# Two of four weight sums per head by accumulating DMAs, and the head loop in another order

## The chip, the cores and the metric

The kernel runs on one core of one Trainium2 chip, as a single program. The metric is the time of one execution on the device in microseconds; before the change the median of three runs is 1553.36 us (1551.82 to 1553.9). Engines are called PE (TensorE, matrix products), DVE (VectorE), ACT (ScalarE), POOL (GpSimd, which here only queues DMAs) and SP (SyncE, which queues nearly all DMAs). All hold their instructions in order and wait for each other with semaphores.

## The reference

A decoder trunk of two layers over 256 positions and a width of 2048, batch 1, in float32. Layer 0 is a multi-scale retention layer (8 heads), layer 1 a pooling mixer with four window widths; each is followed by a gated embedding, and a final RMSNorm ends it. The change touches layer 0 alone, and there the input projection and the work of a head:

```
q, k, v, g = split(rms_norm(x) @ w_in)          # per head 256 + 256 + 512 + 512 columns of w_in
q, k = rotate(q), rotate(k) / 16
y = (q k^T * decay) v                           # causal, decay per head
y = (y - mean(y)) / sqrt(var(y) + 1e-5)         # per head and position
h = x + (silu(g) * y) @ w_out                   # per head 512 rows of w_out
```

## The kernel before

All weights stream from memory once, as units of 128 partitions x 1024 values (512 KB; two blocks of 128 x 512). To keep float32 accuracy on PE, every unit is split: ACT casts it to float32r (`w_hi`, function `head_hi` in the head loop), DVE subtracts that from the original (`w_lo`, `head_lo`), and PE makes three products for each pair of blocks (hi x hi, hi x lo, lo x hi). `w_hi` and `w_lo` are rings of four units: the cast of unit u waits until PE has used unit u-4 (`unit_used`), the subtraction waits for the cast, PE waits for the subtraction (`lo_ready`).

Heads 1 to 7 are a loop of seven passes with 40 units each, in the order of the list `ORDER` (line 80). Four kinds of units are plain products: A (q and k columns; the first four, `h0` to `h3`, are half units), C (v columns), B (gate columns) and O (the output projection of the head before). A full unit has 12 matmuls of 128 x 512. The v and gate products over the first half of the inner dimension are made by a seven-product (Strassen-like) scheme, M1 to M7, each in two parts a and b with 6 matmuls. Their weights are blocks called X1 to X4, and for some products sums of such blocks: M1 uses X1, M3 X3, M2 X4; M5 uses X1+X2, M6 that plus X3, M4 that plus X4, and M7 X2+X3. There are thus four pairs (a, b) of sums per head, eight adds, all made by DVE into two buffers `t1_raw` and `t3_raw` (`t1_sum` to `t4_sum`, line 1235 and on; the arithmetic stands in `quad_sum`, line 1237).

Each pass loads 32 units (`HEAD_LOADS`, line 86: name, one of eight 512 KB slots, and the last unit that reads the slot). SP queues them in that order (`head_loads`, line 417); each load waits until the `w_lo` of the last reader of its slot's former content is done. Ahead of two named loads (`Y_TURN` and `QK_TURN`, line 93) SP queues the DMA transposes of the gated output y and of the rotated q and k ("turns"). ACT writes 16-bit halves for a turn (`y_halves`, `qk_halves`) and puts the transposed halves together afterwards (`y_words`, `qk_words`, which also cast to `oT_hi` and `qkT_hi`).

Where each piece of a head's own work stands among the units is written out by hand, as tests `if u == ...` in the functions `head` of ACT (line 1073) and DVE (line 1560); the order of PE's products stands in PE's `head` (line 635). What the prediction follows: `rotate` (rotary embedding of q, k out of PSUM), `fix_w`, `fix_c` and `fix_b` (what the seven products leave to add or subtract), `v_hi_part` and `v_lo_part` (v out of PSUM; the latter releases `c_read`, for which the output unit O2 waits, line 681), `scores` (line 576, waits for `qkT_ready`), `values`, `normalise` and `gate_y`.

Of the kernel before, what the change touches and what calls it, by code (L numbers as in the profile page):

```python
# [35 lines left out]
TT = 2  # L36
# [43 lines left out]
ORDER = ("h0 h1 h2 h3 A2 M1a A3 M1b A4 M3a A5 M3b A6 M5a A7 M5b "  # L80
         "C4 M6a C5 M6b C6 M7a C7 M7b O0 M4a O1 M4b B4 M2a M2b O2 O3 O4 O5 O6 O7 B5 B6 B7").split()
AT = {name: u for u, name in enumerate(ORDER)}
HEAD_S = len(ORDER)
IN_HEADS = (HEADS - 1) * HEAD_U // (2 * RAW)
MORE = (HEADS - 1) * (HEAD_S - HEAD_U)
HEAD_LOADS = (("A0", 3, "h1"), ("A1", 0, "h3"), ("A2", 1, "A2"), ("X1a", 2, "M1b"), ("X2a", 3, "M3b"), ("A3", 4, "A3"), ("X1b", 5, "M3a"),
# [4 lines left out]
SLOT = {name: slot for name, slot, _last in HEAD_LOADS}  # L91
LOADS_OF = {b: [name for name, slot, _last in HEAD_LOADS if slot == b] for b in range(2 * RAW)}
Y_TURN, QK_TURN = "C4", "O2"
SUM_OF = {"M5": 0, "M6": 4, "M7": 2, "M4": 6}
SUMS = 2 * FORMS
O_RET = -NC
# [35 lines left out]
def trunk(nc, stream, first0, first1, second, third, fourth, x, xT, pT, gains, pool_scale, final_gain, rope, decay, wider, counts, ident, out):  # L132
    with ExitStack() as ctx:
# [3 lines left out]
        def sem(name):  # L137
            return ctx.enter_context(nc.semaphore(name))
# [63 lines left out]
        v_lo = at("v_lo", 36, [P, TT, COL], F32R)  # L202
        t1_raw = at("t1_raw", 32, [P, UNIT, UNIT * COL], F32)
        t3_raw = at("t3_raw", 24, [P, UNIT, UNIT * COL], F32)
        snap_s1 = at("snap_s1", 46, [P, COL], F32)
# [89 lines left out]
        c_read = sem("c_read")  # L295
        t_ready = sem("t_ready")
        snap_ready = sem("snap_ready")
        c_fixed = sem("c_fixed")
# [44 lines left out]
        def load_of(name):  # L343

            if name[0] == "h":
                return f"A{int(name[1]) // 2}"
            if name[0] == "M":
                return {"M1": "X1", "M3": "X3", "M2": "X4"}[name[:2]] + name[2]
            return name

        def unit_raw(name):

            if name[0] == "h":
                return slot(SLOT[load_of(name)])[:, int(name[1]) % 2 * COL:(int(name[1]) % 2 + 1) * COL]
            if name[:2] == "M7":
                return t3_raw[:, "ab".index(name[2]), :]
            if name[:2] in ("M5", "M6", "M4"):
                return t1_raw[:, "ab".index(name[2]), :]
            return slot(SLOT[load_of(name)])
# [105 lines left out]
        @block.gpsimd  # L465
        def _(pool):
            pool.wait_ge(xT_landed[NC - 1], 16)
            pool.dma_start(idn[:], ident).then_inc(idn_landed, 16)
            pool.dma_start(gain[:], gains).then_inc(gain_landed, 16)
            pool.dma_start(pscale[:], pool_scale).then_inc(pscale_landed, 16)  # L470

            pool.wait_ge(rope_landed, 32)
            pool.dma_start(dec[:], decay).then_inc(dec_landed, 16)
            pool.dma_start(p_raw, pT).then_inc(p_landed, 16)

            pool.wait_ge(yT_done, 1)
            pool.dma_start(wide[:], wider).then_inc(inv_landed, 16)
            pool.dma_start(inv[:], counts).then_inc(inv_landed, 16)

            pool.wait_ge(d_ready, 2 * GROUPS)  # L480
            pool.dma_start(fgain[:], final_gain).then_inc(fgain_landed, 16)
# [3 lines left out]
        def _(pe):  # L485
# [149 lines left out]
            def head(hd, base):  # L635
# [40 lines left out]
                g_unit(4, base)  # L676
                product_part("M2a", base, acc["B"][0][:], *a12, False)
                product_part("M2b", base, acc["B"][0][:], *a12, False)
                pe.wait_ge(snap_ready, hd * 3)
# [11 lines left out]
                pe.wait_ge(b_fixed, hd * 2)  # L691
                g_unit(5, base)
                g_unit(6, base)
# [135 lines left out]
        def _(act):  # L829
# [11 lines left out]
            def head_hi(hd, u, base):  # L841

                name = ORDER[u]
                act.wait_ge(unit_used, base + (u + 1 - RING))
                if name[:2] not in SUM_OF and name not in ("h1", "h3"):
                    wait_head_landed(act, hd, load_of(name))
                if name[:2] in SUM_OF:
                    act.wait_ge(t_ready, hd * SUMS + (SUM_OF[name[:2]] + "ab".index(name[2]) + 1 - SUMS))
                dst = w_hi[:, u % RING, 0:COL] if u < HALVES else w_hi[:, u % RING, :]
                act.copy(dst, unit_raw(name)).then_inc(hi_ready, 1)  # L850
# [98 lines left out]
            def qk_words(hd, base):  # L949
                act.wait_ge(yT_ready, hd)  # L950
                words_of(hd * 2 - 1, in_emb, words)
                act.wait_ge(words_ready, hd * 4)
                act.wait_ge(lo_ready, base + (AT["M7b"] + 1))
                for b in range(2):
                    act.copy(qkT_hi[:, 2 * b:2 * b + 2, :], words[:, 2 * b:2 * b + 2, :]).then_inc(qkT_hi_ready, 1)
# [117 lines left out]
            def head(hd, base):  # L1073
                for u in range(HEAD_S):
                    head_hi(hd, u, base)
                    if u == 3:
                        g_sigmoid(hd - 1, base)
                    if u == 6:
                        y_halves(hd - 1)
                    if ORDER[u] == "A6":  # L1080
                        snapshot(snap_s1, base + (AT["M1b"] + 1))
                    if u == 14:
                        y_words(hd - 1)
                    if u == 21:
                        qk_halves(hd)
                    if ORDER[u] == "C7":
                        snapshot(snap_u2, base + (AT["M6b"] + 1))
                    if u == 25:
                        qk_words(hd, base)
                    if u == 26:  # L1090
                        snapshot(snap_u3, base + (AT["M7b"] + 1))
                    if u == 30:
                        act.wait_ge(lo_ready, base + (AT["M4b"] + 1))
                        act.wait_ge(c_fixed, hd * 2)
                        v_hi_part(hd, base + (AT["C7"] + 1))
# [129 lines left out]
        def _(dve):  # L1225
# [12 lines left out]

            def t1_sum(hd, i):
                ab = "ab"[i]  # L1240
                wait_head_landed(dve, hd, "X1" + ab)
                wait_head_landed(dve, hd, "X2" + ab)
                quad_sum(hd, t1_raw[:, i, :], slot(SLOT["X1" + ab]), slot(SLOT["X2" + ab]))

            def t3_sum(hd, i):
                ab = "ab"[i]
                wait_head_landed(dve, hd, "X3" + ab)
                quad_sum(hd, t3_raw[:, i, :], slot(SLOT["X2" + ab]), slot(SLOT["X3" + ab]))

            def t2_sum(hd, i, base):  # L1250
                dve.wait_ge(lo_ready, base + (AT[("M5a", "M5b")[i]] + 1))
                quad_sum(hd, t1_raw[:, i, :], t1_raw[:, i, :], slot(SLOT[("X3a", "X3b")[i]]))

            def t4_sum(hd, i, base):
                dve.wait_ge(lo_ready, base + (AT[("M6a", "M6b")[i]] + 1))
                wait_head_landed(dve, hd, ("X4a", "X4b")[i])
                quad_sum(hd, t1_raw[:, i, :], t1_raw[:, i, :], slot(SLOT[("X4a", "X4b")[i]]))

# [121 lines left out]
            def rotate(hd, done, a_reads, tiles=range(TT)):  # L1380
# [15 lines left out]
                if TT - 1 not in tiles:  # L1396
                    return
                ins.then_inc(a_read, 1)
                dve.wait_ge(a_read, a_reads)
                dve.tensor_tensor(qk[:], qk[:], qk2[:], ALU.add).then_inc(qk_ready, 1)  # L1400
# [159 lines left out]
            def head(hd, base):  # L1560
                for u in range(HEAD_S):
                    head_lo(u, base)
                    if u == 4:
                        gate_y(hd - 1)
                    if u in (6, 8):
                        t1_sum(hd, (u - 6) // 2)
                    if u in (10, 12):
                        t3_sum(hd, (u - 10) // 2)
                    if u in (14, 16):
                        t2_sum(hd, (u - 14) // 2, base)  # L1570
                    if u in (22, 24):
                        t4_sum(hd, (u - 22) // 2, base)
                    if u == 21:
                        y_lo_part(hd - 1, False)
                    if u in (18, 19):
                        rotate(hd, base + (AT["A7"] + 1), hd * 3 - 1, (u - 18,))
                    if u == 26:
                        qkT_lo_part(hd, False)
                    if u == 28:
                        fix_w(hd, base)  # L1580
                    if u == 29:
                        fix_c()
                    if u == 31:
                        v_lo_part(hd)
# [319 lines left out]
```

## Time and profile before

| what | us |
|---|---|
| median of three runs | 1553.36 |
| the profiled execution | 1553.85 |
| its span, from first to last instruction | 1551.6 |
| PE busy | 1531.0 |
| DVE busy | 1153.2 |
| ACT busy | 926.6 |
| POOL busy | 4.6 |
| one pass of the head loop (259.00 to 348.43) | 89.43 |

The profile is of one execution, and its times are its own; it took 0.49 us more than the median of the runs. PE's busy time counts pipelined matmuls, whose ends are modelled, so small delays are best read from the starts of successive matmuls in the timeline. The seven passes of the head loop lie between 78.80 and some 705 us. PE's granted clock is 1.00 in every stretch of the head loop.

### The profile page before, as it was taken

What the parts mean: (1) busy time and instruction counts of PE and PEld (TensorE: products, weight loads), DVE (VectorE), ACT (ScalarE), POOL (GpSimd) and SP (SyncE); (2) the same over time, 40 slices, a digit from 0 to 9 for tenths busy, and PEclk for the clock granted to TensorE, in tenths of its full rate; (3) what the DMA queues carried; (4) which work ended last, traced back from release to release, by engine and by line L of the source; (5) the groups of instructions that cost most, each with busy time, mean ns of one, the idle gap of its engine ahead of it and who ended that gap; (6) DMA issues with size and microseconds to landing.
All of it is one profiled execution on the core that took longest, in us unless ns stands there. A gap on an engine that the chain in (4) does not pass through costs nothing.

```text
span 1551.6 us, 19968 instructions
## 1 busy us (share of the span) xinstructions
PE 1531.0 (99%) x6788; PEld 1259.3 (81%) x6788; DVE 1153.2 (74%) x1418; ACT 926.6 (60%) x1108; POOL 4.6 (0%) x12
## 2 busy tenths in 40 slices
PE   9999999999999999999999999999999999999997
PEld 7777878888887888888888888888888888888885
DVE  6989888888979888997766675775577557755665
ACT  7466574747566474756767556644664476446843
POOL 0000000000000000000000000000000000000000
PEclk9999999999999999999999999999999999999998
DMA  9485665757666565765566657655765576555651
GB/s 383 162 255 181 208 200 186 203 174 232 202 215 187 181 201 193 217 212 200 194 206 228 199 208 210 224 197 196 222 213 200 189 216 219 216 204 186 219 195 74
DMA packets 133498, 318.42 MB, mean 205 GB/s; under 512 B 80545, under 2 KB 80561, under 8 KB 112337
## 3 DMA queue, kind: packets, MB, share of 16 engines
q1 hardware_dynamic: 132608, 314.35, 60.9%
q0 software_dynamic: 704, 3.27, 0.5%
q8 instruction: 25, 0.41, 0.1%
q10 hardware_dynamic: 144, 0.26, 0.0%
q14 instruction: 17, 0.13, 0.0%
HBM read 297.40 MB, written 2.10 MB: 193 GB/s over the span
## 4 chain that ended last, share of the span: by engine, by line
PE 75%; DVE 10%; issue 6%; ACT 4%; DMA 4%; SPq 1%; ACTq 0%; DVEq 0%
PE accA L493 9%; PE accA L494 9%; PE accA L495 9%; PE accC L493 9%; PE accC L494 8%; PE accC L495 8%; PE accB L493 5%; PE accB L494 5%; PE accB L495 5%; DVE w_lo L1232 3%; DMA halvesT_e<-halves_e 2%; DMA w_raw<-in_stream_dram 2%; ACT w_hi L850 1%; ACT words_e L929 1%; DVE t_raw L1237 1%
## 5 line engine op out<-in xcount | busy, mean ns | idle before, releaser
L1311 DVE TENSOR_TENSOR w_lo<-w_raw,w_hi 128x1024 fp32r<-128x1024 f32 x326 | 395.8, 1222 | 227.8 <-ACT w_hi L839 226.0
L839 ACT CAST w_hi<-w_raw 128x1024 fp32r<-128x1024 f32 x326 | 340.0, 1052 | 267.9 <-PE accA L495 100.7
L850 ACT CAST w_hi<-w_raw 128x1024 fp32r<-128x1024 f32 (+1 forms) x224 | 219.5, 998 | 166.2 <-PE accC L495 50.5
L1232 DVE TENSOR_TENSOR w_lo<-w_raw,w_hi 128x1024 fp32r<-128x1024 f32 (+1 forms) x224 | 255.4, 1152 | 61.1 <-ACT w_hi L850 60.4
L493 PE MATMUL accA<-w_hi,xa_hi 128*128 128x512 f32 x452 | 176.2, 390 | 1.0 <-DVE w_lo L1311 0.6
L495 PE MATMUL accA<-w_hi,xa_lo 128*128 128x512 f32 x452 | 175.9, 389 | 0.0
L494 PE MATMUL accA<-w_lo,xa_hi 128*128 128x512 f32 x452 | 175.9, 389 | 0.0
L493 PE MATMUL accC<-w_hi,xa_hi 128*128 128x512 f32 x396 | 155.0, 391 | 0.5 <-DVE w_lo L1232 0.2
L494 PE MATMUL accC<-w_lo,xa_hi 128*128 128x512 f32 x396 | 154.2, 389 | 0.0
L495 PE MATMUL accC<-w_hi,xa_lo 128*128 128x512 f32 x396 | 154.1, 389 | 0.0
L493 PEld LDWEIGHTS accA<-w_hi,xa_hi 128*128 128x128 f32 x452 | 84.8, 188 | 19.7 <-DVE w_lo L1232 1.1
L495 PEld LDWEIGHTS accA<-w_hi,xa_lo 128*128 128x128 f32 x452 | 84.8, 188 | 17.6
L494 PEld LDWEIGHTS accA<-w_lo,xa_hi 128*128 128x128 f32 x452 | 84.8, 188 | 17.5
L493 PEld LDWEIGHTS accC<-w_hi,xa_hi 128*128 128x128 f32 x396 | 74.3, 188 | 18.9 <-DVE w_lo L1232 3.4
L495 PEld LDWEIGHTS accC<-w_hi,xa_lo 128*128 128x128 f32 x396 | 74.3, 188 | 15.6
L494 PEld LDWEIGHTS accC<-w_lo,xa_hi 128*128 128x128 f32 x396 | 74.3, 188 | 15.2
L1232 DVE TENSOR_TENSOR w_lo<-t_raw,w_hi 128x1024 fp32r<-128x1024 f32 x56 | 68.3, 1219 | 14.0 <-ACT w_hi L850 14.0
L493 PE MATMUL accC<-w_hi,oT_hi 128*128 128x512 f32 x184 | 72.4, 394 | 5.5 <-DVE v_lo L1423 5.5
L493 PE MATMUL accA<-w_hi,oT_hi 128*128 128x512 f32 x184 | 72.4, 394 | 0.2
L494 PE MATMUL accC<-w_lo,oT_hi 128*128 128x512 f32 x184 | 71.7, 390 | 0.0
L495 PE MATMUL accC<-w_hi,oT_lo 128*128 128x512 f32 x184 | 71.7, 390 | 0.0
L495 PE MATMUL accA<-w_hi,oT_lo 128*128 128x512 f32 x184 | 71.6, 389 | 0.0
(277 smaller groups left out, 2947.4 us busy)
## 6 DMA issues: line engine op xcount, KB each, us to landing
w_raw<-in_stream_dram SPq DMA_DIRECT2D x162, 1024.0 KB, 4.8
w_raw<-in_stream_dram SPq DMA_DIRECT2D x224, 512.0 KB, 4.9
h<-in_x_dram SPq DMA_DIRECT2D x4, 512.0 KB, 13.3
xT_raw<-in_xT_dram SPq DMA_DIRECT2D x3, 512.0 KB, 14.4
dec<-in_decay_dram POOLq DMA_DIRECT2D x1, 1024.0 KB, 9.2
fgain<-in_final_gain_dram POOLq DMA_DIRECT2D x1, 1024.0 KB, 7.1
out_dram<-emb SPq DMA_DIRECT2D x1, 1024.0 KB, 3.8
halvesT_e<-halves_e SPq DMA_TRANSPOSE x56, 6.1
```

The costliest lines, as they stand in the source:

```text
L493: pe.matmul(acc[pair][t][:, 0:n], xh, wh, start=first and b == 0, stop=False, skip_group_check=onto)
L494: pe.matmul(acc[pair][t][:, 0:n], xh, wl, start=False, stop=False, skip_group_check=onto)
L495: mm = pe.matmul(acc[pair][t][:, 0:n], xl, wh, start=False, stop=last and b == UNIT - 1, skip_group_check=onto)
L839: act.copy(w_hi[:, r % RING, :], w_raw[:, r // 2, (r % 2) * 1024:(r % 2 + 1) * 1024]).then_inc(hi_ready, 1)
L850: act.copy(dst, unit_raw(name)).then_inc(hi_ready, 1)
L929: act.copy(dst[:].bitcast(U16).rearrange("p k (n two) -> p two k n", two=2)[:, i, :, :], bufs[1][:, 4 * i:4 * i + 4, :]).then_inc(words_re ...
L1232: dve.tensor_tensor(w_lo[:, u % RING, 0:n], unit_raw(ORDER[u]), w_hi[:, u % RING, 0:n].bitcast(F32), ALU.subtract).then_inc(lo_ready, 1)
L1237: dve.tensor_tensor(dst, in0, in1, ALU.add).then_inc(t_ready, 1)
L1311: dve.tensor_tensor(w_lo[:, r % RING, :], w_raw[:, r // 2, (r % 2) * 1024:(r % 2 + 1) * 1024], w_hi[:, r % RING, :].bitcast(F32), ALU.subt ...
```

## The change

Two of the four pairs of sums are no longer made by DVE. POOL queues four DMAs a head that add a block from memory onto a block that lies in its slot: X2 onto X1 (a and b, once M1 has used X1) for M5, and X3 onto X2 (once X2 has landed) for M7. DVE makes the other two pairs in place: X3 onto the X1 slots for M6, and X4 for M4. `t1_raw` and `t3_raw` go, and so two waits of ACT that guarded their memory. The stream's blocks are ordered anew with `HEAD_LOADS`, the slots are given out anew, both turns stand at other loads, PE makes B5 ahead of M2b, and many pieces of ACT's and DVE's head work stand at other units.

```
-         "C4 M6a C5 M6b C6 M7a C7 M7b O0 M4a O1 M4b B4 M2a M2b O2 O3 O4 O5 O6 O7 B5 B6 B7").split()
+         "C4 M6a C5 M6b C6 M7a C7 M7b O0 M4a O1 M4b B4 M2a B5 M2b O2 O3 O4 O5 O6 O7 B6 B7").split()
-HEAD_LOADS = (("A0", 3, "h1"), ("A1", 0, "h3"), ("A2", 1, "A2"), ("X1a", 2, "M1b"), ("X2a", 3, "M3b"), ("A3", 4, "A3"), ("X1b", 5, "M3a"),
...
+HEAD_LOADS = (("A0", 3, "h1"), ("A1", 2, "h3"), ("A2", 1, "A2"), ("X1a", 0, "M4a"), ("A3", 3, "A3"), ("X1b", 6, "M4b"), ("A4", 5, "A4"),
+              ("X3a", 4, "M5b"), ("A5", 7, "A5"), ("X3b", 2, "M6a"), ("A6", 1, "A6"), ("X2a", 3, "M7a"), ("A7", 5, "A7"), ("X2b", 7, "M7b"),
+              ("C4", 1, "C4"), ("C5", 5, "C5"), ("C6", 4, "C6"), ("C7", 1, "C7"), ("X4a", 2, "M2a"), ("X4b", 5, "M2b"), ("O0", 4, "O0"),
+              ("O1", 3, "O1"), ("B4", 1, "B4"), ("B5", 4, "B5"), ("O2", 0, "O2"), ("O3", 1, "O3"), ("O4", 2, "O4"), ("O5", 3, "O5"), ("O6",
+              4, "O6"), ("O7", 5, "O7"), ("B6", 6, "B6"), ("B7", 7, "B7"))
-Y_TURN, QK_TURN = "C4", "O2"
-SUM_OF = {"M5": 0, "M6": 4, "M7": 2, "M4": 6}
+Y_TURN, QK_TURN = "C5", "B4"
+DMA_SUM = {"M5": "X1", "M7": "X2"}
+SUM_OF = {"M6": 0, "M4": 2}
@@ POOL
+            def add_block(hd, base, x, term, used):
+                n = names.index(term + x[2])
+                at = hd * (HEAD_U // (2 * RAW)) + ((RET1 - HEAD_U + n) // (2 * RAW))
+                pool.wait_ge(lo_ready, base + (AT[used] + 1))
+                pool.dma_start(slot(SLOT[x]), rounds[at, n // 2 % RAW, :, n % 2 * UNIT * COL:(n % 2 + 1) * UNIT * COL],
+                               accum_op=ALU.add).then_inc(sum_landed[x], 16)
+            def head_sums(hd, base):
+                add_block(hd, base, "X1a", "X2", "M1a")
+                add_block(hd, base, "X1b", "X2", "M1b")
+                wait_head_landed(pool, hd, "X2a")
+                add_block(hd, base, "X2a", "X3", "M1b")
+                wait_head_landed(pool, hd, "X2b")
+                add_block(hd, base, "X2b", "X3", "M1b")
@@ PE, head
                 product_part("M2a", base, acc["B"][0][:], *a12, False)
+                g_unit(5, base)
                 product_part("M2b", base, acc["B"][0][:], *a12, False)
...
-                g_unit(5, base)
@@ ACT, head_hi
+                if name[:2] in DMA_SUM:
+                    act.wait_ge(sum_landed[DMA_SUM[name[:2]] + name[2]], hd * 16)
@@ ACT, head: the unit behind which each piece stands
-  g_sigmoid 3, y_halves 6, y_words 14, qk_halves 21, qk_words 25, v_hi_part 30
+  g_sigmoid 4, y_halves 8, y_words 19, qk_halves 23, qk_words 28, v_hi_part 29
@@ DVE, head: the same
-  gate_y 4, t1_sum 6 and 8, t3_sum 10 and 12, rotate 18 and 19, y_lo_part 21, qkT_lo_part 26, fix_w 28, fix_c 29, v_lo_part 31
+  gate_y 6, rotate 17 and 19, its sum (rotated) 20, y_lo_part 23, qkT_lo_part 31, fix_w 27, fix_c 28, v_lo_part 30
```

The last four lines put the diff's tests `if u == ...` in a row. `t2_sum` (behind units 14 and 16) and `t4_sum` (22 and 24) stay at their places and now add in place into the X1 slots.

## Rows read from the trace of the kernel before

**Rows 1.** The page: one engine's busy time (1), the main DMA queue (3).
```profile
PE 1531.0 (99%) x6788; PEld 1259.3 (81%) x6788; DVE 1153.2 (74%) x1418; ACT 926.6 (60%) x1108; POOL 4.6 (0%) x12
...
q1 hardware_dynamic: 132608, 314.35, 60.9%
```
**Rows 2.** Stretches: length, busy, clock, DMA share, GB/s; five heads' sum.
```profile
900.00:1000.00 100.00, 100.00 (x443) 82.81 (x442) 63.71 (x66) 60.82 (x67) 0.00 (x0) 1.00 0.66 213
...
259.00:348.43 89.43, 88.55 (x394) 72.71 (x393) 77.52 (x98) 54.07 (x60) 0.00 (x0) 1.00 0.63 199
...
sum 446.93, PE 442.74 PEld 363.59 DVE 387.78 ACT 270.40 POOL 0.00; mean PE 88.55 PEld 72.72 DVE 77.56 ACT 54.08 POOL 0.00
```
**Rows 3.** PE's waits: line, waited for, us in total, times, longest.
```profile
PE accC L493 <- DVE v_lo L1423: 5.5, 7, 0.8
```
**Rows 4.** Timeline of PE, head 259.00: start, duration, line, operation (before C6, O1, O2).
```profile
287.56 0.39 PE L525 MATMUL side<-w_hi,f_hi 128*128 128x512 f32 x1
...
288.92 0.39 PE L493 MATMUL accC<-w_hi,xa_hi 128*128 128x512 f32 x1
...
296.85 0.39 PE L527 MATMUL side<-w_hi,f_lo 128*128 128x512 f32 x1
297.28 0.50 PE L493 MATMUL accC<-w_hi,xa_hi 128*128 128x512 f32 x1
...
309.43 0.39 PE L527 MATMUL accB<-w_hi,xa_lo 128*128 128x512 f32 x1
309.85 0.50 PE L493 MATMUL accA<-w_hi,oT_hi 128*128 128x512 f32 x1
...
320.73 0.28 PE L586 MATMUL side<-qkT_hi,qkT_lo 128*128 128x128 f32 x1
321.81 0.49 PE L493 MATMUL accC<-w_hi,oT_hi 128*128 128x512 f32 x1 [0.80 <-DVE v_lo L1423]
```
**Rows 5.** Timeline of DVE, same head: an add, and O1's subtraction.
```profile
268.05 1.22 DVE L1237 TENSOR_TENSOR t_raw<-w_raw 128x1024 f32<-128x1024 f32 x1
...
308.57 1.23 DVE L1232 TENSOR_TENSOR w_lo<-w_raw,w_hi 128x1024 fp32r<-128x1024 f32 x1 [2.20 <-ACT w_hi L850]
```
**Rows 6.** Timeline of ACT, same head.
```profile
287.83 1.06 ACT L850 CAST w_hi<-w_raw 128x1024 fp32r<-128x1024 f32 x1 [0.68 <-PE accA L495]
...
296.12 2.00 ACT L919 COPY halves_e<-qk 128x1024 uint16<-128x1024 uint16 x2 [1.80 <-DVE qk L1400]
...
303.74 2.60 ACT L929 COPY words_e<-halvesT_e 128x1024 uint16<-128x1024 uint16 x2 [0.82 <-DMA halvesT_e<-halves_e]
...
307.50 1.04 ACT L850 CAST w_hi<-w_raw 128x1024 fp32r<-128x1024 f32 x1
...
316.89 1.27 ACT L910 ACTIVATE v_hi<-accC,rs 128x512 fp32r<-128x512 f32 x2 [2.93 <-DVE accC L1299]
318.05 3.88 ACT L850 CAST w_hi<-w_raw 128x1024 fp32r<-128x1024 f32 x4
```
**Rows 7.** Line 432, the head's plain loads (35 issued between 268 and 362 us).
```profile
DMA to landing us min/median/max: 3.5/4.8/7.6
```
**Rows 8.** The page (6): loads from POOL's queue, KB each, us to landing.
```profile
fgain<-in_final_gain_dram POOLq DMA_DIRECT2D x1, 1024.0 KB, 7.1
...
sig<-in_pT_dram POOLq DMA_DIRECT2D x1, 512.0 KB, 12.3
```
**Rows 9.** Timeline of SP, same head: the two turns, each with the load behind it.
```profile
272.23 1.26 SPq L414 DMA_TRANSPOSE halvesT_e<-halves_e  x1
...
278.18 1.54 SPq L432 DMA_DIRECT2D w_raw<-in_stream_dram  x3
...
298.21 1.24 SPq L414 DMA_TRANSPOSE halvesT_e<-halves_e  x1
...
301.93 0.38 SPq L432 DMA_DIRECT2D w_raw<-in_stream_dram  x1
```
**Rows 10.** Groups of DVE, same head: busy, mean ns, idle before and its releaser.
```profile
L1232 DVE TENSOR_TENSOR w_lo<-w_raw,w_hi 128x1024 fp32r<-128x1024 f32 (+1 forms) x32 | 36.4, 1151 | 9.0 <-ACT w_hi L850 8.9
```

More of the change, by code:

```diff
@@ L85 @@
 MORE = (HEADS - 1) * (HEAD_S - HEAD_U)
-HEAD_LOADS = (("A0", 3, "h1"), ("A1", 0, "h3"), ("A2", 1, "A2"), ("X1a", 2, "M1b"), ("X2a", 3, "M3b"), ("A3", 4, "A3"), ("X1b", 5, "M3a"),
[4 rows of a table removed]
+HEAD_LOADS = (("A0", 3, "h1"), ("A1", 2, "h3"), ("A2", 1, "A2"), ("X1a", 0, "M4a"), ("A3", 3, "A3"), ("X1b", 6, "M4b"), ("A4", 5, "A4"),
[4 rows of a table added]
 SLOT = {name: slot for name, slot, _last in HEAD_LOADS}
 LOADS_OF = {b: [name for name, slot, _last in HEAD_LOADS if slot == b] for b in range(2 * RAW)}
-Y_TURN, QK_TURN = "C4", "O2"
-SUM_OF = {"M5": 0, "M6": 4, "M7": 2, "M4": 6}
-SUMS = 2 * FORMS
+Y_TURN, QK_TURN = "C5", "B4"
+DMA_SUM = {"M5": "X1", "M7": "X2"}
+SUM_OF = {"M6": 0, "M4": 2}
+SUMS = 4
 O_RET = -NC
@@ L202, in trunk @@
         v_lo = at("v_lo", 36, [P, TT, COL], F32R)
-        t1_raw = at("t1_raw", 32, [P, UNIT, UNIT * COL], F32)
-        t3_raw = at("t3_raw", 24, [P, UNIT, UNIT * COL], F32)
         snap_s1 = at("snap_s1", 46, [P, COL], F32)
@@ L296, in trunk @@
         t_ready = sem("t_ready")
+        sum_landed = {x: sem(f"sum_landed_{x}") for x in ("X1a", "X1b", "X2a", "X2b")}
         snap_ready = sem("snap_ready")
@@ L347, in load_of @@
             if name[0] == "M":
-                return {"M1": "X1", "M3": "X3", "M2": "X4"}[name[:2]] + name[2]
+                return {"M1": "X1", "M5": "X1", "M6": "X1", "M4": "X1", "M7": "X2", "M3": "X3", "M2": "X4"}[name[:2]] + name[2]
             return name
@@ L354, in unit_raw @@
                 return slot(SLOT[load_of(name)])[:, int(name[1]) % 2 * COL:(int(name[1]) % 2 + 1) * COL]
[L355 to L358, printed above, removed]
             return slot(SLOT[load_of(name)])
@@ L466, in _ @@
         def _(pool):
+            rounds = stream.rearrange("(i s) p n -> i s p n", s=RAW)
+            names = [name for name, _slot, _last in HEAD_LOADS]
+            def add_block(hd, base, x, term, used):
[11 more added lines that the diff above has]
+                add_block(hd, base, "X2b", "X3", "M1b")
             pool.wait_ge(xT_landed[NC - 1], 16)
@@ L474, in _ @@
             pool.dma_start(p_raw, pT).then_inc(p_landed, 16)
+            for hd in range(1, HEADS):
+                head_sums(hd, hd * HEAD_S + (RET1 - HEAD_S))
             pool.wait_ge(yT_done, 1)
@@ L844, in head_hi @@
                 act.wait_ge(unit_used, base + (u + 1 - RING))
-                if name[:2] not in SUM_OF and name not in ("h1", "h3"):
+                if name[:2] not in SUM_OF and name[:2] not in DMA_SUM and name not in ("h1", "h3"):
                     wait_head_landed(act, hd, load_of(name))
+                if name[:2] in DMA_SUM:
+                    act.wait_ge(sum_landed[DMA_SUM[name[:2]] + name[2]], hd * 16)
                 if name[:2] in SUM_OF:
@@ L952, in qk_words @@
                 act.wait_ge(words_ready, hd * 4)
-                act.wait_ge(lo_ready, base + (AT["M7b"] + 1))
                 for b in range(2):
@@ L1075, in head @@
                     head_hi(hd, u, base)
-                    if u == 3:
+                    if u == 4:
                         g_sigmoid(hd - 1, base)
-                    if u == 6:
+                    if u == 8:
                         y_halves(hd - 1)
@@ L1081, in head @@
                         snapshot(snap_s1, base + (AT["M1b"] + 1))
-                    if u == 14:
+                    if u == 19:
                         y_words(hd - 1)
-                    if u == 21:
+                    if u == 23:
                         qk_halves(hd)
@@ L1087, in head @@
                         snapshot(snap_u2, base + (AT["M6b"] + 1))
-                    if u == 25:
+                    if u == 28:
                         qk_words(hd, base)
@@ L1091, in head @@
                         snapshot(snap_u3, base + (AT["M7b"] + 1))
-                    if u == 30:
-                        act.wait_ge(lo_ready, base + (AT["M4b"] + 1))
+                    if u == 29:
                         act.wait_ge(c_fixed, hd * 2)
@@ L1237, in quad_sum @@
                 dve.tensor_tensor(dst, in0, in1, ALU.add).then_inc(t_ready, 1)
[L1239 to L1248, printed above, removed]
             def t2_sum(hd, i, base):
                 dve.wait_ge(lo_ready, base + (AT[("M5a", "M5b")[i]] + 1))
-                quad_sum(hd, t1_raw[:, i, :], t1_raw[:, i, :], slot(SLOT[("X3a", "X3b")[i]]))
+                x1 = slot(SLOT[("X1a", "X1b")[i]])
+                quad_sum(hd, x1, x1, slot(SLOT[("X3a", "X3b")[i]]))
             def t4_sum(hd, i, base):
@@ L1256, in t4_sum @@
                 wait_head_landed(dve, hd, ("X4a", "X4b")[i])
-                quad_sum(hd, t1_raw[:, i, :], t1_raw[:, i, :], slot(SLOT[("X4a", "X4b")[i]]))
+                x1 = slot(SLOT[("X1a", "X1b")[i]])
+                quad_sum(hd, x1, x1, slot(SLOT[("X4a", "X4b")[i]]))
             def form_sums(i):
@@ L1398, in rotate, with rotated @@
                 ins.then_inc(a_read, 1)
+                if len(tiles) == TT:
+                    rotated(a_reads)
+            def rotated(a_reads):
                 dve.wait_ge(a_read, a_reads)
@@ L1562, in head @@
                     head_lo(u, base)
-                    if u == 4:
+                    if u == 6:
                         gate_y(hd - 1)
[L1565 to L1568, printed above, removed]
                     if u in (14, 16):
@@ L1572, in head @@
                         t4_sum(hd, (u - 22) // 2, base)
-                    if u == 21:
+                    if u in (17, 19):
+                        rotate(hd, base + (AT["A7"] + 1), hd * 3 - 1, ((u - 17) // 2,))
+                    if u == 20:
+                        rotated(hd * 3 - 1)
+                    if u == 23:
                         y_lo_part(hd - 1, False)
-                    if u in (18, 19):
-                        rotate(hd, base + (AT["A7"] + 1), hd * 3 - 1, (u - 18,))
-                    if u == 26:
+                    if u == 31:
                         qkT_lo_part(hd, False)
+                    if u == 27:
+                        fix_w(hd, base)
                     if u == 28:
-                        fix_w(hd, base)
-                    if u == 29:
                         fix_c()
-                    if u == 31:
+                    if u == 30:
                         v_lo_part(hd)
```

4 rows, old and new, of the table HEAD_LOADS are left out of this document.

## The prediction

> **What bounds the kernel now.** I read the page's first part first: TensorE (PE) is busy for 99% of the span [rows 1]. The table by stretches shows where the rest is: a stretch of the pool stage has no idle PE, while five heads of the head loop take 446.93 us, 89.39 each, with PE idle about 1% [rows 2]. PE's list of waits has one long row, 5.5 us in seven pieces, for `v_lo` of VectorE (DVE) [rows 3]. The timeline of PE in the head from 259.00 to 348.43 shows the losses. Where nothing is late a matmul starts every 0.227 us (six in 1.36) [rows 4]. At C6 the first matmul starts 0.43 after the one ahead of it, 0.20 late, and takes 0.50 in place of 0.39: 0.31 us. At O1 it is 0.19 and 0.11: 0.30. At O2, behind the scores' short matmuls (0.11 apart), 0.97 and 0.10: 1.07. That is 1.68 us in a head that is as long as the mean, 11.8 us in seven heads, and all that this change can win: 0.76% of the run. DVE as a whole is not short of time (77.5 of 89.4 us), but each gap ends on it, or on ScalarE (ACT), which feeds it.
>
> **What it removes.** Per head eight adds on DVE (`t_raw`) become four; each takes DVE 1.22 us [rows 5], so it has 4.9 us less to do. That pays only where a gap waits for DVE; PE's own work is unchanged.
>
> *O2's gap.* `fix_c` stood behind unit 29, `v_hi` behind cast 30, `v_lo` behind unit 31, the one just ahead of O2, and PE waited for its end. Each now stands a unit earlier, and B5, M2b and the scores lie between: `v_lo` follows the `w_lo` of B5, when PE has B5 (2.72), M2b (1.36) and the scores (1.3) still to do. It is two operations of half a unit's size; up to 5 us would be hidden. `qkT_lo`, now behind unit 31, is as large and has M2b's 1.36 of cover: just in time for the scores. I take the whole 1.07 as won.
>
> *O1's gap.* ACT made the qk words (303.74 to 307.50) ahead of O1's cast; the cast started at 307.50, its `w_lo` at 308.57, PE at 309.85 [rows 4 to 6]. The words now come behind cast 28. Heads differ here; I take 0.25 as won.
>
> **What it adds: 28 accumulating DMAs of 512 KB from POOL's queue.** The trace has none. From below: a plain load of that size lands 3.5 us after issue at the least. From above: POOL's `sig` load, stuck behind others, took 12.3 [rows 7, 8]. I take 7.1, that of POOL's 1 MB load, since an add has to read the old block and the addend. The first pair has least time. X1a's add starts when the `w_lo` of M1a is done, some 6 us after the head's start, and lands at 13. Unit starts follow from 1.36 and 2.72 a unit, and a cast starts 0.27 after the successor of the unit that frees its ring slot (287.83 against 287.56 [rows 4, 6]): cast M5a may start at 18.0, M5b at 22.0, where X1b's add, from 11, lands at 18. PE is held only by a cast that starts later than 2.35 before its unit (1.07 to `w_lo`, 1.28 to PE), so 12.3 costs nothing either; some 15 us are the limit. The adds of X2a and X2b have more. Behind their waits only each other is queued.
>
> The Trainium skill (Collectives: The Full Stack, "The bandwidth ceiling: the fold count and why AG ≠ RS ≠ AR") says that a DMA that adds reads two sources through one ring and so moves at half a copy's rate. By it the sum stays as it is, and the engines pay twice a load for each add; no run here shows it yet.
>
> **The y turn and C6.** Here I expect the change to pay something back. Times from the head's start: cast A6 waits for A4's matmuls (16.33), starts at 16.6, its `w_lo` ends at 18.9, and only then does SP issue C4's load, at 19.0, and the y turn, at 19.6. (Before, the turn began at 13.2, 272.23.) Its two transposes hold SP for 5.95 us (272.23 to 278.18), those of the qk turn 3.72 (298.21 to 301.93) [rows 9]. So C5 is issued between 23.3 and 25.6 and, with the median of 4.8 [rows 7], lands between 28.1 and 30.4. Behind it ACT casts C5 and M6b (0.95 each), makes y's words as it makes qk's (3.76), then casts C6: PE can start C6 0.1 + 1.9 + 3.76 + 2.35 = 8.1 after C5's landing. Without a gap its turn is at 38.1, so C5 must land by 30.0. The quick turn gives no gap, the slow one 0.4 and the restart's 0.1. I take 0.56 (C5 at 30.5), 0.25 more than now: nearer to the slow turn, since two loads and an add are in flight ahead of it.
>
> **B5.** From the end of O0: 0.27, cast B4 0.95, qk's words 3.76, cast M2a 0.95, `v_hi` 1.16, then 2.35, in sum 9.4. PE has M4a, O1, M4b, B4 and M2a, 9.5, until it wants B5. There is no slack, and B4's load now stands behind the qk turn. From C5's landing at 30.5 ACT has six casts, y's words, a snapshot of half a cast's size and the qk halves (2.0 [rows 6]): to 42.4. The turn's 3.72 and a landing of 4.8 give 50.9; the cast could have started at 49.6 + 0.56 + 0.27 = 50.4. I take 0.35 lost; the range is 0 to 0.9.
>
> The other moves (gate, y halves, rotation in two parts, later O units) lie beside units for which DVE has time to spare (ahead of its `w_lo` it waits 9.0 us a head, 8.9 of them for ACT's casts [rows 10]); I cost them at nothing. If that lead is gone, PE waits for `w_lo` between A4 and M5b.
>
> **Sum.** Per head -1.07 - 0.25 + 0.25 + 0.35 = -0.72; in seven -5.0 us. The profiled execution took 1553.85 us (span 1551.6 and 2.25 around it): 1548.8. It lies 0.49 above the median of the runs: 1548.3.
>
> **Rivals.** (1) *C5 lands late, because the adds share the DMA engines with the turn: slower.* X2b lands at 20 to 22; its add then runs until 27 to 30, over the transposes and C5's load. The loads' queue took 60.9% of the span for 314.35 MB [rows 1], 1.6 us for 512 KB; an add of twice that takes 3.2. If C5 bears half of it, the gap grows by 1.6, if all, by 3.2: -0.72 + 1.6 = +0.88 a head, 1559.5, or +2.48, 1570.7; between them 1565. It decides from C5 at 31.2 on. For: landings reach 7.6 [rows 7], and a turn can last 2.2 us longer than another. Against: the engines are idle for over a third of the span, and X2b's add is not wanted before 39.
>
> The Trainium skill (DMA: Bandwidth & Descriptors, "Issuing engines are not separate DMA queues") speaks for it: what POOL queues runs interleaved on the engines that serve SP's loads.
>
> (2) *It cancels*: C5 at 31.2, and what O2 gains comes back at C6 and B5. 1553, within 3.
> (3) *The sums are late.* An add over 15 us, or one behind another for so long, holds cast M5a or M5b; each us costs seven. With 3 us a head and the forecast's other terms: 1569. Against: the longest seen is 12.3, in the crowded start.
> (4) *Nothing is lost at C6 or B5*: -1.68 a head, 1541.6; the forecast's lower edge.
>
> **How the numbers follow.** A measurement of this kernel tells about 0.2% (3.1 us) from no change. Forecast with (4) 0.47, (2) 0.19, (1) 0.27, (3) 0.07: faster 0.47, same 0.19, slower 0.34. The likeliest case alone has 1541.6 to 1550; with the others 1542 to 1566, which leaves out the upper parts of (1) and (3).
>
> **What would show it.** Right: PE's waits have no `v_lo` row, 28 `t_raw` adds are left, C6 has a gap of 0.3 to 0.8, O1 none, a head takes 88.7 us. Rival 1 shows as ACT waiting for `w_raw` at C5's cast and a gap over 1.2 at C6 or at C5 itself; rival 3 as a wait of cast M5a or M5b for an add. I am wrong if a head takes longer than 89.4, or if an accumulating DMA takes far more than 7 us to land.

## The result and the profile after

The changed kernel takes 1567.0 us (median of seven runs, 1559.02 to 1572.67) against 1553.36 (1551.82 to 1553.99): a ratio of 1.0079, 95% interval 1.0054 to 1.0105. It is slower by 13.6 us where 5 us faster were forecast, and its runs lie 13.6 us apart, those of before 2.2. The profiled execution took 1568.04 us, with a span of 1566.0.

The page of the changed kernel (engines' busy time; DMA queues with packets, MB and share of 16 engines; issues with KB each and us to landing) answers to [rows 1] and [rows 8]:

```profile
PE 1531.3 (98%) x6788; PEld 1261.6 (81%) x6788; DVE 1124.6 (72%) x1390; ACT 926.2 (59%) x1108; POOL 28.8 (2%) x40
...
q1 hardware_dynamic: 132608, 314.35, 60.5%
q0 software_dynamic: 4736, 17.95, 5.6%
...
w_raw<-in_stream_dram POOLq DMA_DIRECT2D x28, 512.0 KB, 8.3
```

DVE has 28.6 us less to do, as intended. PE's work is the same, the span 14.4 us longer. PE's list of waits in the changed kernel answers to [rows 3]; behind it stands one row of ACT's list:

```profile
PE accC L512 <- DVE w_lo L1251: 19.8, 8, 7.4
```
```profile
ACT w_hi L871 <- DMA w_raw<-in_stream_dram: 71.3, 24, 12.0
```

The `v_lo` row is gone. A longer one has come: eight waits before v units, up to 7.4 us, for a `w_lo` that waits for a cast, which waits for a load (12.0 us at the longest). Six heads one by one show where (length, PE, PEld, DVE, ACT, POOL busy; granted clock, DMA share, GB/s), and a last stretch just behind the first long wait; they answer to [rows 2]:

```profile
78.04:177.87 99.83, 90.97 (x393) 74.59 (x394) 74.59 (x96) 53.48 (x60) 3.47 (x4) 0.97 0.75 201
177.87:274.78 96.91, 89.52 (x394) 73.67 (x393) 73.45 (x94) 53.89 (x60) 3.43 (x4) 0.96 0.76 206
274.78:363.93 89.15, 88.33 (x394) 72.74 (x393) 73.46 (x94) 53.82 (x60) 3.45 (x4) 1.00 0.74 223
363.93:453.96 90.03, 88.67 (x395) 72.66 (x393) 73.46 (x94) 53.82 (x60) 3.45 (x4) 1.00 0.73 222
453.96:542.92 88.96, 88.38 (x395) 72.74 (x393) 73.45 (x94) 53.91 (x60) 3.46 (x4) 1.00 0.73 224
542.92:631.60 88.68, 88.16 (x395) 72.74 (x393) 73.45 (x94) 53.85 (x60) 3.45 (x4) 1.00 0.74 225
121.30:127.00 5.70, 5.47 (x13) 4.37 (x14) 3.86 (x6) 5.35 (x6) 0.00 (x0) 0.52 0.47 161
```

Heads 3 to 6 lie within 1.4 us of the forecast's 88.7; heads 1 and 2 take 99.8 and 96.9. PE's timeline in head 1 shows the loss, at C4 and C5 (start, duration; it answers to the C6 rows of [rows 4]):

```profile
107.90 0.39 PE L546 MATMUL side<-w_hi,f_lo 128*128 128x512 f32 x1
110.35 0.50 PE L512 MATMUL accC<-w_hi,xa_hi 128*128 128x512 f32 x1 [2.07 <-DVE w_lo L1251]
...
114.34 0.39 PE L546 MATMUL side<-w_hi,f_lo 128*128 128x512 f32 x1
121.53 0.80 PE L512 MATMUL accC<-w_hi,xa_hi 128*128 128x512 f32 x1 [6.80 <-DVE w_lo L1251]
122.12 0.63 PE L513 MATMUL accC<-w_lo,xa_hi 128*128 128x512 f32 x1
...
126.78 0.40 PE L544 MATMUL side<-w_hi,f_hi 128*128 128x512 f32 x1
```

C4 starts 2.45 after the matmul ahead of it, 2.2 late, and C5 7.19 after, 7.0 late. Then C5's twelve matmuls take 5.25 us (121.53 to 126.78) in place of 2.72: the granted clock of that stretch is 0.52, the lower of the two levels (1.2 GHz), after 7 us in which PE stood still. Together 11.7 us. Head 2 has the same at C5, 9.1 us with its half clock.

Why C5's load is late stands in the timeline of SP, in head 1 and, below the dots, in head 2 (it answers to [rows 9]), in that of POOL and in that of ACT (casts of A6 and of C5, both in head 1):

```profile
99.94 0.33 SPq L428 DMA_DIRECT2D w_raw<-in_stream_dram  x1
100.47 6.20 SPq L410 DMA_TRANSPOSE halvesT_e<-halves_e  x2
106.93 6.14 SPq L428 DMA_DIRECT2D w_raw<-in_stream_dram  x4
...
197.46 9.25 SPq L410 DMA_TRANSPOSE halvesT_e<-halves_e  x2
206.96 20.70 SPq L428 DMA_DIRECT2D w_raw<-in_stream_dram  x7
```
```profile
99.31 0.86 POOL L471 DMA_DIRECT2D w_raw<-in_stream_dram  x1 [8.96 <-DMA w_raw<-in_stream_dram]
101.75 0.85 POOL L471 DMA_DIRECT2D w_raw<-in_stream_dram  x1 [1.59 <-DMA w_raw<-in_stream_dram]
```
```profile
97.46 1.05 ACT L871 CAST w_hi<-w_raw 128x1024 fp32r<-128x1024 f32 x1 [2.42 <-DMA w_raw<-in_stream_dram]
...
119.17 1.99 ACT L871 CAST w_hi<-w_raw 128x1024 fp32r<-128x1024 f32 x2 [9.18 <-DMA w_raw<-in_stream_dram]
```

The adds into X2a and X2b are issued one on each side of the y turn's first transpose. The DMA view of two stretches of that head, 102 to 107 (issues with us to landing) and 107 to 116 (queues with packets, MB, share of 16 engines):

```profile
w_raw<-in_stream_dram POOLq DMA_DIRECT2D x1, 512.0 KB, 15.5
w_raw<-in_stream_dram SPq DMA_DIRECT2D x1, 512.0 KB, 12.2
halvesT_e<-halves_e SPq DMA_TRANSPOSE x2, 16.1
```
```profile
DMA packets 984, 0.66 MB, mean 74 GB/s; under 512 B 877, under 2 KB 877, under 8 KB 983
...
q1 hardware_dynamic: 862, 0.21, 84.3%
q0 software_dynamic: 121, 0.43, 43.4%
```

Transposes and add crawl together: 16.1 and 15.5 us to landing, 0.66 MB in nine microseconds, while the packets of the two queues take 84.3% and 43.4% of the engines' time. A packet of SP's queue (862 in 0.21 MB, so nearly all are the transposes', of some 250 bytes) takes 0.843 x 16 x 9 / 862 = 0.141 us on the mean. C5, issued at 107 behind the turn in the same queue, lands 12.2 us later, just behind the transposes, and ACT can cast it at 119.2 (41.1 from the head's start). In head 3 the same DMA view (294 to 305) has the turn landing in half the time:

```profile
w_raw<-in_stream_dram POOLq DMA_DIRECT2D x1, 512.0 KB, 7.5
halvesT_e<-halves_e SPq DMA_TRANSPOSE x2, 7.9
```

Yet an add is in flight beside the turn there too: in every head POOL issues the add into X2b 1.3 to 4.1 us after the turn has begun. Head 4 is closest to the two slow heads. The rows of POOL and SP and the DMA view (382 to 388) in head 4:

```profile
382.20 0.87 POOL L471 DMA_DIRECT2D w_raw<-in_stream_dram  x1 [6.11 <-DMA w_raw<-in_stream_dram]
385.62 0.86 POOL L471 DMA_DIRECT2D w_raw<-in_stream_dram  x1 [2.55 <-DMA w_raw<-in_stream_dram]
```
```profile
383.52 6.50 SPq L410 DMA_TRANSPOSE halvesT_e<-halves_e  x2
```
```profile
halvesT_e<-halves_e SPq DMA_TRANSPOSE x2, 8.5
```

Its adds into X2a and X2b are issued 1.3 us ahead of the turn's start and 2.1 behind it, in head 1 1.2 and 1.3, in head 2 0.9 and 2.3. So the meeting slows the turn in every head, and in some it becomes a crawl of 15 to 16 us; what tips it over, the trace does not show.

### The profile page after: what moved, and what is told of

Its sections match the earlier page's. It is cut to its first block, busy times and chain, and to the rows that moved or that the text cites. A ratio compares the mean times of both kernels' runs of the same rounds, so it can differ in the third digit from the quotient of the medians.

```text
span 1566.0 us, 19940 instructions
## 1 busy us (share of the span) xinstructions
PE 1531.3 (98%) x6788; PEld 1261.6 (81%) x6788; DVE 1124.6 (72%) x1390; ACT 926.2 (59%) x1108; POOL 28.8 (2%) x40
## 4 chain that ended last, share of the span: by engine, by line
PE 80%; DMA 6%; ACT 4%; DVE 4%; SPq 4%; issue 2%; ACTq 0%; DVEq 0%
PE accA L512 9%; PE accA L514 9%; PE accA L513 9%; PE accC L512 9%; PE accC L514 9%; PE accC L513 9%; DMA w_raw<-in_stream_dram 6%; PE accB L512 6%; PE accB L514 5%; PE accB L513 5%; SPq L410 3%; ACT w_hi L871 2%; DVE w_lo L1251 1%; ACT words_e L950 1%; PE side L544 1%
## 5 line engine op out<-in xcount | busy, mean ns | idle before, releaser
L871 ACT CAST w_hi<-w_raw 128x1024 fp32r<-128x1024 f32 (+1 forms) x280 | 274.7, 1010 | 233.6 <-DMA w_raw<-in_stream_dram 71.3
L1251 DVE TENSOR_TENSOR w_lo<-w_raw,w_hi 128x1024 fp32r<-128x1024 f32 (+1 forms) x280 | 320.7, 1168 | 110.6 <-ACT w_hi L871 110.6
L512 PE MATMUL accC<-w_hi,xa_hi 128*128 128x512 f32 x396 | 157.0, 396 | 19.9 <-DVE w_lo L1251 19.8
L513 PE MATMUL accA<-w_lo,oT_hi 128*128 128x512 f32 x184 | 71.6, 389 | 0.0
```

What stands on the lines that cost most here:

```text
L512: pe.matmul(acc[pair][t][:, 0:n], xh, wh, start=first and b == 0, stop=False, skip_group_check=onto)
L513: pe.matmul(acc[pair][t][:, 0:n], xh, wl, start=False, stop=False, skip_group_check=onto)
L1251: dve.tensor_tensor(w_lo[:, u % RING, 0:n], unit_raw(ORDER[u]), w_hi[:, u % RING, 0:n].bitcast(F32), ALU.subtract).then_inc(lo_ready, 1)
```

## The experiments

Theory A: time is lost where POOL's adds and the y turn's transposes are in flight together. Rivals: the adds cost engine time wherever they lie (B); any DMA of POOL's queue beside the transposes does it (C); the sums come late (D). The expectations put the long stops at C5 and C6; counted from the head's start they are those of C4 and C5, one unit earlier, and nothing hangs on the name. Each run was timed beside runs of the kernel before on the same chip (medians 1552.65 to 1552.9).

**1. The adds into X2 after the turn.** In `head_sums`:

```
                 add_block(hd, base, "X1b", "X2", "M1b")
+                pool.wait_ge(halvesT_landed, hd * 64 - 32)
                 wait_head_landed(pool, hd, "X2a")
```

> The changed kernel with one wait more: POOL starts the accumulating DMAs into X2a and X2b only when the y turn's transposes of that head have landed. Theory A (the time is lost where accumulating DMAs and the y turn's DMA transposes are in flight together, as in heads 1 and 2, where both took 14 to 17 us instead of 7 to 9): the two long stops of heads 1 and 2 (2.2 + 7.0 + 2.4 us and 7.6 + 1.6 us with the half clock behind them) go, the turn lands in 7 us or less in every head, 1546 to 1552 us, and the runs lie within 4 us of each other. Theory B (the adds simply cost engine time, two reads for one, wherever they lie): nothing to gain from a later start, 1562 to 1572. Theory D (the sums come late for M7a and M7b now): ScalarE waits for them, 1 to 3 us a head, 1555 to 1570, with the stop in front of M7a and not at C5 or C6.

Measured: 1545.01 us (1541.67 to 1546.03), ratio 0.9944 (0.993 to 0.9958). PE's long row falls from 19.8 us to 0.5, its DMA work unchanged:

```profile
PE accC L513 <- DVE w_lo L1252: 0.5, 1, 0.5
```

One wait on POOL gives 22 us (1567.0 to 1545.0). As A says, even a little better; B and D fall. The turn of head 1 lands in 4.6 us; the runs lie 4.4 us apart, a little more than the 4 that A allowed. What is left of small gaps lies in head 1 (3.4 us).

**2. Copies in place of adds.** `accum_op=ALU.add` is taken out of `add_block`.

> The changed kernel with its 28 accumulating DMAs as plain copies of the same blocks at the same places (so the products M5, M6, M4 and M7 take wrong weights: the sums with X2 and X3 are left out, the instructions and bytes written are the same). Theory A (it is the accumulating that collides with the transposes): packets of 159 ns instead of 327 ns, no long stop, 1543 to 1552. Rival C (any DMA of POOL's queue beside the transposes does it): the long stops at C5 and C6 stay in some heads, 1558 to 1570. Theory B (engine time alone): half of the adds' surplus goes, 1553 to 1560 without any stop that is longer than 3 us.

Measured: 1548.24 us (1542.64 to 1551.45), ratio 0.9965 (0.9953 to 0.9977). In A's range, but not free of C: PE's row is 4.5 us, with stops of 2.2, 1.2 and 1.1.

```profile
PE accC L512 <- DVE w_lo L1251: 4.5, 3, 2.2
```

**3. The adds into X2 with the turn.**

```
                 wait_head_landed(pool, hd, "X2a")
+                pool.wait_ge(turn_begun, hd * 2 - 1)
                 add_block(hd, base, "X2a", "X3", "M1b")
```

> The changed kernel with one wait more: POOL starts the accumulating DMA into X2a (and with it that into X2b) when SP has begun the y turn of that head, so that they are in flight beside its transposes in all 7 heads and not in two. Theory A: a stop of 6 to 10 us in front of C5, C6 or C7 in 5 to 7 heads and the half clock behind it, 1595 to 1630. Theory B: the same engine time, 1560 to 1572. If only an add that is already under way when the transposes start collides, the time falls instead, to 1550 to 1556.

Measured: 1608.28 us (1604.97 to 1625.66), ratio 1.039 (1.0339 to 1.0441). The time is in A's range, and now all seven heads stop at C5, by 3.2 to 11.0 us; A had 6 to 10, and only two of the seven lie in that.

```profile
PE accC L513 <- DVE w_lo L1252: 46.5, 7, 11.0
```

Between this kernel and that of experiment 1 the bytes and instructions are the same, and only the start of 14 DMAs differs: 63 us. The last sentence of the expectation (only an add already under way collides) falls.

**4. Copies with the turn** (edits 2 and 3 together).

> The kernel that holds the DMAs into X2a and X2b back until the y turn begins, with its 28 accumulating DMAs as plain copies (so the sums with X2 and X3 are left out and the products take wrong weights). It tells whether it is the accumulating or POOL's queue alone that stalls beside the transposes. Theory A (accumulating): the seven stops of 3.4 to 11.1 us at C6 shrink to under 1.5 us each, 1544 to 1555 us. Rival C (any transfer of a second queue beside the transposes): stops of 3 us or more stay in most heads, 1570 to 1605. Between these (a copy packet costs half and the stops halve): 1558 to 1570, and then the time goes with the engines' time and not with the kind of packet.

Measured: 1566.28 us (1564.88 to 1569.67), ratio 1.009 (1.0075 to 1.0106). That is between A and C, in the band that was put down to the engines' time.

```profile
PE accC L513 <- DVE w_lo L1252: 16.2, 10, 4.9
```

**5. Twice the copies with the turn.** In `add_block` of kernel 4 (and the casts of M7a and M7b wait for both):

```
+                if x[:2] == "X2":
+                    pool.dma_start(dead[:, "ab".index(x[2]), :],
+                                   rounds[at, n // 2 % RAW, :, n % 2 * UNIT * COL:(n % 2 + 1) * UNIT * COL]
+                                   ).then_inc(sum_landed[x], 16)
```

> The kernel whose plain copies into X2a and X2b are held back until the y turn begins (1566.3 us; the sums with X2 and X3 are left out), with each of these copies made twice: the second goes into a buffer that is dead there. POOL's queue then moves 4 copies beside each turn, whose engine time is that of the 2 accumulating DMAs of the kernel with 1608.3 us. If it is the engines' time in the second queue that stretches the turn, whatever the kind of packet: 1590 to 1625. If the accumulating itself does it beyond its time: the stops grow little, 1566 to 1580. In between, 1580 to 1590, both have a part.

Measured: 1590.12 us (1585.32 to 1596.7), ratio 1.0229 (1.0212 to 1.0246), on the border of two bands.

```profile
PE accC L518 <- DVE w_lo L1257: 40.3, 9, 8.7
```

Against the kernel without any DMA of POOL in the heads (1540.74, experiment 8) two copies beside each turn cost 25.5 us, four 49.4, two adds 67.5 (each with the X1 transfers too, which cost 1.4 by experiment 6). Twice the copies cost twice as much, so the loss grows with what POOL's queue moves while the transposes run; engine time, bytes and packets double together here and are not told apart. Two adds cost 18 us more than four copies, whose engine time is nearly the same (4 x 159 against 2 x 327 ns a packet), so adding has a part of its own. A's place is shown, and its claim that the adding is what collides is not: C is right that a plain copy there does it too, and an add costs some two and a half times a copy.

**6. One pair of sums by DMA.** The X2 adds of POOL are taken out, and DVE adds in place:

```
+            def t3_sum(hd, i):
...
+                x2 = slot(SLOT[("X2a", "X2b")[i]])
+                quad_sum(hd, x2, x2, slot(SLOT[("X3a", "X3b")[i]]))
...
+                    if u in (13, 15):
+                        t3_sum(hd, (u - 13) // 2)
```

> The changed kernel with only X1 += X2 by accumulating DMA (14 of the 28); X2 += X3 is added in place by VectorE (1.22 us each, 14 more) at units 13 and 15 of a head, where VectorE waited 1.3 to 1.5 us for ScalarE. Theory A: no accumulating DMA is left near the y turn, no long stop, 1544 to 1552, runs within 4 us. Theory B: half of the adds' engine time is left, halfway between 1545 and 1567: 1554 to 1560. If VectorE's 1.22 us before units 14 and 16 is not covered, w_lo comes late there: up to 2.4 us a head, 1562 to 1570.

Measured: 1542.17 us (1541.22 to 1542.39), ratio 0.9928 (0.9914 to 0.9941). That is A, 2 us below its range; the runs lie 1.2 us apart. The X1 adds, in flight beside plain loads alone, cost next to nothing.

**7. VectorE's work put back.** In `head_lo` of kernel 6:

```
+                if u in (8, 10):
+                    dve.wait_ge(lo_ready, base + u)
+                    dve.tensor_tensor(sig[:].rearrange("p t n -> p (t n)"), unit_raw(ORDER[u]), w_hi[:, u % RING, 0:n].bitcast(F32),
+                                      ALU.subtract)
```

> The kernel with X1 += X2 by accumulating DMA and X2 += X3 by VectorE, and 14 more VectorE instructions of 128 x 1024 (a subtraction like that of w_lo, into a buffer that is dead there, ahead of that of units 8 and 10 of each head, its result unused): VectorE's work is that of the kernel before again, in the new order. If the gain of 10.5 us comes from the order of loads, products and head work alone, nothing moves: 1541 to 1545. If it comes from the time that VectorE was freed of, it goes back by up to 14 x 1.22 = 17 us: 1550 to 1559. If half of it is covered by VectorE's waits for ScalarE: 1545 to 1550.

Measured: 1542.37 us (1541.36 to 1543.16), ratio 0.9932 (0.9918 to 0.9945). DVE is busy for 1154.1 us, as before the change (1153.2), and nothing moves. What DVE was relieved of was worth nothing.

**8. All sums by VectorE, in the new order.** POOL's part of the head loop goes; beside `t3_sum` as in 6:

```
-              ("X3a", 4, "M5b"), ("A5", 7, "A5"), ("X3b", 2, "M6a"), ("A6", 1, "A6"), ("X2a", 3, "M7a"), ("A7", 5, "A7"), ("X2b", 7, "M7b"),
-              ("C4", 1, "C4"), ("C5", 5, "C5"), ("C6", 4, "C6"), ("C7", 1, "C7"), ("X4a", 2, "M2a"), ("X4b", 5, "M2b"), ("O0", 4, "O0"),
+              ("X3a", 4, "M5b"), ("A5", 7, "A5"), ("X3b", 2, "M6a"), ("X2a", 3, "M7a"), ("A6", 1, "A6"), ("X2b", 5, "M7b"), ("A7", 7, "A7"),
+              ("C4", 1, "C4"), ("C5", 7, "C5"), ("C6", 4, "C6"), ("C7", 1, "C7"), ("X4a", 2, "M2a"), ("X4b", 7, "M2b"), ("O0", 4, "O0"),
...
+                    if u in (10, 12):
+                        t1_sum(hd, (u - 10) // 2)
```

> No accumulating DMA at all: the order of the changed kernel with all four pair sums made in place by VectorE (X1 += X2 at units 10 and 12, X2 += X3 at units 13 and 15, the rest as it is); X2a and X2b are loaded one and one place earlier, in front of A6 and A7, and X2b and A7 change buffers. If order is what gains: 1541 to 1546, with 14.7 MB less read from memory. If the accumulating DMA is needed for the gain: 1550 to 1560. If X2b or A7 lands late in the new places: ScalarE waits for it at M5b or A7, 0.5 to 1.5 us a head, 1546 to 1553.

Measured: 1540.74 us (1540.5 to 1541.48), ratio 0.9922 (0.9909 to 0.9936): the fastest of all, 12.2 us below the kernel before and 26.3 below the changed one. The same table of its heads has no idle PE and no lost clock; of its six heads, the first and the third:

```profile
78.56:166.49 87.93, 87.93 (x393) 73.00 (x394) 78.76 (x100) 53.75 (x60) 0.00 (x0) 1.00 0.64 204
...
254.30:342.05 87.75, 87.75 (x394) 72.90 (x393) 77.61 (x98) 54.05 (x60) 0.00 (x0) 1.00 0.65 203
```

And its y turn lands in 4.8 us (DMA view, 273 to 278: SP's queue, then the turn), in the kernel before in 6.6 (the same view, 272 to 278):

```profile
q1 hardware_dynamic: 937, 0.75, 75.0%
...
halvesT_e<-halves_e SPq DMA_TRANSPOSE x2, 4.8
```
```profile
halvesT_e<-halves_e SPq DMA_TRANSPOSE x2, 6.6
```

## Why the prediction was wrong

*The terms that were won are right.* O2 and O1 no longer wait. In head 5 of the changed kernel's timeline of PE, the rows that answer to those of O1 and O2 in [rows 4]:

```profile
504.64 0.39 PE L546 MATMUL accB<-w_hi,xa_lo 128*128 128x512 f32 x1
504.86 0.39 PE L512 MATMUL accA<-w_hi,oT_hi 128*128 128x512 f32 x1
...
518.94 0.28 PE L605 MATMUL side<-qkT_hi,qkT_lo 128*128 128x128 f32 x1
519.06 0.45 PE L512 MATMUL accC<-w_hi,oT_hi 128*128 128x512 f32 x1
```

O1 starts 0.22 behind its predecessor in place of 0.42, O2 0.12 in place of 1.08. Without the adds near the turn C6 and B5 lose nothing either: in kernel 8 a head takes 87.80 us on the mean of six, 1.59 less than the 89.39 of [rows 2], and seven such are 11.1 of the 12.2 us that it gains. That is close to the sum of the gaps that the prediction read (1.68 a head) and to its rival 4 (1541.6). It comes from the order of loads, products and head work as a whole, whose moves were not tried one by one; relief of DVE has no part in it (experiment 7).

*The step that failed is C5's landing behind the y turn.* The prediction put it at 30.5 from the head's start: a turn begun at 19.6 that holds SP for 5.95 us at most [rows 9], then 4.8 us to landing, the median of the plain loads [rows 7]. Those rows are of a kernel in which POOL's queue moves nothing in the heads, and for the overlap with the adds the sum took no more than the slow turn. In head 1 C5 came at 41.1. The turn began at 22.4, 2.8 us late, since ACT had waited 2.4 us for A6's load, which was in flight beside the add into X1b; the turn held SP for 6.5 us; and C5 took 12.2 us to land, which is 7.4 of the 10.6 us. In head 2 the turn began at 19.6, as forecast, but held SP for 9.5 us. The turn itself took 16.1 us to land in head 1, against 4.8 in kernel 8. The terms for C6 (a gap of 0.56) and B5 (0.35) were sized on the same turn: in heads 3 to 6, where the turn is quicker, C6 is late by 0.4 to 1.3 us and B5 by at most 0.5, and without adds beside the turn neither is (kernel 8). The sum for B5 also has a slip: it sets the end of O0 at 49.6, where its own unit lengths give 38.1 + 10.9 = 49.0, so by its own rows the term should have been some 0.6 larger.

*Rival 1 named the place and the direction, and was mis-sized.* It priced sharing by the engines' time, 3.2 us for an add, half or all of it borne by C5 in each head. That its middle of 1565 lies near the 1567.0 is luck: 9 to 12 us came in each of two heads, and some 1 to 2 in the others. Its arithmetic holds for an add beside plain loads. In a stretch of head 1 (90 to 97) with an add and loads, whose queues the DMA view gives as

```profile
q0 software_dynamic: 245, 0.94, 67.1%
q1 hardware_dynamic: 278, 1.02, 38.4%
```

4 KB of an add take 0.671 x 16 x 7 / (0.94 MB / 4 KB) = 0.33 us of an engine, 4 KB of a load 0.17. The Trainium skill (Collectives: The Full Stack, "The bandwidth ceiling: the fold count and why AG ≠ RS ≠ AR") says of the adding step of a ReduceScatter that it reads two sources through one ring and so runs at half a copy's rate; for an add into SBUF on one core this trace agrees, 0.33 us against 0.17. What the price left out is that packets stretch where add and transposes meet: in the crawl of head 1 the transposes' packets take 0.14 us (in kernel 8 those of SP's queue take 0.75 x 16 x 5 / 937 = 0.06, larger loads among them) and the add's 0.434 x 16 x 9 / 121 = 0.52 in place of 0.33. The turn, with the loads behind it in SP's queue, gets longer by 11 us, more than three times the 3.2 that an add was priced at. It does so in two heads of this execution; in the other heads whose turns are shown, where an add meets the turn as well, it lands in 7.9 and 8.5 us. With 9 to 12 us a crawl, and another number of them in each execution, the runs' spread of 13.6 us would follow; that was not counted in other executions, but in kernels 6 and 8, where the X2 adds and the turn can't meet, it is 1.2 and 1.0.

*The adds themselves.* 7.1 us to landing was taken, 8.3 is the median, 15.5 beside the turn. No cast of M5 waited long enough to stop PE, so rival 3 did not come.

What stays open is why the packets stretch, and why a meeting becomes a crawl in one head and not in the next. In the crawl the packets' times add up to 128% of the engines' time while 74 GB/s move; no run here tells what a packet waits for.

## What to carry to other kernels

Before a transfer is put on a second queue, look for transfers of small packets (here DMA transposes) in the same stretch, and order the two with a wait: one wait on the queue that is not urgent turned 1567 into 1545 us. A price in bytes or engine time, taken from rows in which the two never met, is no upper bound. And relieve an engine only where a gap waits for it: the whole gain here was the order, and the fastest kernel is the one with the new order and without the new DMAs.

## What the runs showed of the hardware

- A turn of two DMA transposes (packets of some 250 bytes) lands in 4.8 us (kernel 8) or 6.6 (kernel before) with loads alone beside it, and beside accumulating DMAs in 16.1 us in head 1 but in 7.9 and 8.5 in heads 3 and 4; the add beside the slow turn takes 15.5 us in place of a median of 8.3.
- Plain copies on the second queue, held back to run beside the turn, do the same to a smaller degree: two a head cost 25.5 us over seven heads, four 49.4, two adds 67.5.
- After a stop of 7.0 us PE ran at a granted clock of 0.52 for some 5 us, which added 2.5 us to the stop.
